# An earlier router, a shared bias split and one more weight place in a hybrid attention and mixture-of-experts block

## The reference

```python
h = x
h = h + hybrid_mixer(rms_norm(h, norm_mix_g), w_in, ..., w_out)   # two attentions, gated, then @ w_out
hn = rms_norm(h, norm_ffn_g)                                     # [256, 1024]
h = h + moe_ffn(hn, w_router, b_router, w_gate_up, b_gate_up, w_down, b_down)

def moe_ffn(xf, ...):
    logits = xf @ w_router + b_router                            # [256, 32]
    top_vals, top_idx = lax.top_k(logits, 4)
    gates = softmax(top_vals)
    # for each expert e, on the tokens that chose it:
    hgu = xb @ w_gu[e] + b_gu[e]                                 # 1024 -> 2048
    gate, up = min(hgu[:, :1024], 7), clip(hgu[:, 1024:], -7, 7)
    y = ((up + 1) * gate * sigmoid(1.702 * gate)) @ w_down[e] + b_down[e]
    # the gate-weighted y is added to the rows of its tokens
```

## Time and profile before

| | |
|---|---|
| median of 3 runs | 1224.87 us (1224.17 to 1225.32) |
| the profiled execution's own time | 1224.58 us |
| its span in the profile | 1223.0 us |
| PE busy | 1146.1 us (94%) |
| DVE busy | 277.8 us (23%) |
| ACT busy | 113.1 us (9%) |
| POOL busy | 33.0 us (3%) |
| moved by DMA | 435.75 MB, mean 356 GB/s |

### The profile page before, as it was taken

One profiled execution on the slowest core, in us unless ns is written; L12 is line 12 of the kernel. 1 busy time (PEld: TensorE's weight loads), 2 busy tenths in 40 slices (PEclk: granted clock), 3 DMA queues, 4 the chain that ended last, 5 costly groups with the idle time before them and its releaser, 6 DMA issues.

```text
span 1223.0 us, 12848 instructions
## 1 busy us (share of the span) xinstructions
PE 1146.1 (94%) x5681; PEld 553.6 (45%) x5681; DVE 277.8 (23%) x590; ACT 113.1 (9%) x206; POOL 33.0 (3%) x23
## 2 busy tenths in 40 slices
PE   6959999979999999999999978999999999999996
PEld 3656878554444444444444324444443333333331
DVE  1297332332111112221111111211111111111111
ACT  1102542010000000000000000000000000000000
POOL 1170000000000000000000000000000000000000
PEclk9979999968999999999999997999999999999999
DMA  7535336367999999999999999999999999999994
GB/s 231 168 138 216 129 138 275 142 275 292 373 418 417 417 418 416 418 417 417 417 417 417 417 417 417 416 418 417 417 417 417 417 417 417 416 417 417 417 417 199
DMA packets 87560, 435.75 MB, mean 356 GB/s; under 512 B 8688, under 2 KB 9872, under 8 KB 54640
## 3 DMA queue, kind: packets, MB, share of 16 engines
q1 hardware_dynamic: 87376, 434.83, 87.9%
q0 software_dynamic: 96, 0.08, 0.2%
q10 hardware_dynamic: 32, 0.01, 0.0%
HBM read 433.84 MB, written 1.05 MB: 356 GB/s over the span
## 4 chain that ended last, share of the span: by engine, by line
PE 63%; DMA 25%; DVE 4%; SPq 3%; issue 2%; ACT 1%; POOL 0%; DVEq 0%; POOLq 0%
PE Pp L682 25%; DMA ring<-in_w_gate_up 16%; PE Bp L697 12%; PE Bp L669 7%; DMA qkv<-in_w_gate_up 6%; PE Pp L456 5%; PE Pp L444 4%; PE Ap L711 3%; SPq L317 3%; PE Pp L609 2%; DMA XT<-in_w_gate_up 2%; PE Ap L620 1%; PE Pp L676 1%; PE Bp L689 1%; DVE ring L891 1%
## 5 line engine op out<-in xcount | busy, mean ns | idle before, releaser
L682 PE MATMUL Pp<-ring,OBT 128*64 128x512 f32 x1360 | 308.9, 603 | 14.4 <-DMA ring<-in_w_gate_up 14.4
L682 PEld LDWEIGHTS Pp<-ring,OBT 128*64 128x64 f32 x1360 | 95.6, 138 | 214.3 <-issue 166.0
L1086 DVE TENSOR_SCALAR G<-Pp 128x512 f32<-128x512 f32 x32 | 22.1, 691 | 674.1 <-PE Pp L682 674.1
L697 PE MATMUL Bp<-ring,G 128*64 128x512 f32 x688 | 152.8, 596 | 0.9 <-DVE G L1097 0.9
L669 PEld LDWEIGHTS Bp<-cst,XR 128*128 128x128 f32 x1024 | 122.6, 199 | 31.0 <-issue 31.0
L669 PE MATMUL Bp<-cst,XR 128*128 128x64 f32 x1024 | 127.2, 285 | 5.4 <-issue 4.4
L697 PEld LDWEIGHTS Bp<-ring,G 128*64 128x64 f32 x688 | 47.5, 137 | 90.7 <-issue 89.7
L456 PE MATMUL Pp<-XT,unit 128*128 128x256 f32 x384 | 85.9, 383 | 0.0
L682 PE MATMUL Pp<-unit,OBT 128*64 128x512 f32 x352 | 78.9, 594 | 2.5 <-DMA unit<-in_w_gate_up 2.4
L456 PEld LDWEIGHTS Pp<-XT,unit 128*128 128x128 f32 x384 | 72.7, 192 | 11.0 <-issue 1.1
L697 PE MATMUL Bp<-unit,G 128*64 128x512 f32 x320 | 70.9, 595 | 0.0
(11 more groups left out here) (191 smaller groups left out, 673.8 us busy)
## 6 DMA issues: line engine op xcount, KB each, us to landing
ring<-in_w_gate_up SPq DMA_DIRECT2D x170, 1024.0 KB, 20.7
ring<-in_w_down SPq DMA_DIRECT2D x86, 1024.0 KB, 25.4
unit<-in_w_gate_up SPq DMA_DIRECT2D x44, 1024.0 KB, 21.2
unit<-in_w_down SPq DMA_DIRECT2D x40, 1024.0 KB, 24.8
qkv<-in_w_gate_up SPq DMA_DIRECT2D x21, 1024.0 KB, 21.0
XT<-in_w_gate_up SPq DMA_DIRECT2D x21, 1024.0 KB, 19.2
unit<-in_w_in SPq DMA_DIRECT2D x8, 2048.0 KB, 7.9
ring<-in_w_out SPq DMA_DIRECT2D x2, 2048.0 KB, 12.9
```

The costliest lines, as they stand in the source:

```text
L682: last = mm((Gps, Ups)[q // 2][64 * (q % 2):64 * (q % 2) + 64, :], xT[:, k, :], w[:, q * 512:(q + 1) * 512], start=False, stop=k == KC - 1 ...
L697: last = mm(Yps[64 * hf:64 * hf + 64, :], hT[:, k % 4, k // 4, :], w[:, half * 1024 + hf * 512:][:, 0:512], start=k == 0, stop=k == KC - 1 ...
L1086: V.tensor_scalar(gm, Gps, LIMIT, None, ALU.min).then_inc(d_gm, 1)
```

## The change

1. **Router on the unnormed sum.** `turn_h` turns X itself, not a normed copy. The gain is multiplied once into the router weights, on POOL (`g_neg` = -0.5 times the gain). The factor of the norm (`nrm`, one number for a token, from `root_correction`, in which the factor -2 is left) is multiplied into the logits and into the one-hot of the gather. ACT alone empties the transposes.
2. **Order.** Block 0 is turned, multiplied by the router weights, routed and ranked between and inside the last out-projections (the fourth is cut in two halves by c); half of its gather follows right behind. `route` finds the chosen experts with `match_replace`; the gates are computed later (`gates`, behind the first `take_expert`), and the rank products use bf16 tables.
3. **Bias split** on ACT (four copies, one over 96 partitions) and DVE (three subtractions), out of `BG`, which is the memory of `XR`, loaded before unit 3. POOL keeps two new small instructions.
4. **One place more.** `BG` becomes place 18 of the ring, and piece (1, 8) is loaded into it right after unit 8. The output is written from X.

```diff
-PLACES = 18
+PLACES = 19
...
+        BG = XR[:, :, :].rearrange("p b n -> p (b n)")
...
+                if u == 2:
+                    sp.wait_ge(m_xt, 2)
+                    for s in range(3):
+                        sp.dma_start(BG[32 * s:32 * s + 32, :], b_gate_up[0]).then_inc(in_b, 16)
                 if u == 3:
-                    for s in range(3):
-                        sp.dma_start(W2[32 * s:32 * s + 32, :], b_gate_up[0]).then_inc(in_b, 16)
...
+                if u == 8:
+                    sp.wait_ge(bias_ok, 2)
+                    load_piece(1, 8)
...
             inverse_root(18, 2)
-            pool.wait_ge(in_b, 48)
...
+            pool.wait_ge(in_c, 16)
+            nc.gpsimd.tensor_copy(tab[:, :, :], strict_ones).then_inc(g_tab, 1)
+            pool.wait_ge(in_r, 16)
+            pool.wait_ge(a_gn, 2)
+            nc.gpsimd.tensor_tensor(WR[:, :, :], WR[:, :, :], g_neg.unsqueeze(2).to_broadcast([P, KC, NE]), ALU.mult)\
+                .then_inc(g_wr, 1)
...
             out_projection(0, 0)
             out_projection(0, 1)
+            turn_h(0, 0)
             out_projection(1, 0)
-            turn_h(0)
-            out_projection(1, 1)
-            router_products(0)
-            turn_h(1)
-            router_products(1)
+            turn_h(0, 1)
+            out_projection(1, 1, 0, 4)
+            pe.wait_ge(g_wr, 1)
+            router_products(0, 0)
+            router_products(0, 1)
+            turn_h(1, 0)
+            out_projection(1, 1, 4, KC)
+            pe.wait_ge(g_tab, 1)
+            pe.wait_ge(v_as, 1)
+            mm(Rps[:, 0, :], before, AS[:, 0, :], start=True, stop=True, skip_group_check=True).then_inc(m_rk, 1)
+            router_products(1, 0)
+            turn_h(1, 1)
+            pe.wait_ge(d_oh, 1)
+            gather_block(Tps, 0, 0, 4)
+            router_products(1, 1)
+            mm(Rps[:, 1, :], every, AS[:, 0, :], start=False, stop=False, skip_group_check=True)
+            mm(Rps[:, 2, :], every, AS[:, 0, :], start=False, stop=False, skip_group_check=True)
+            gather_block(Tps, 0, 4, KC)
+            pe.wait_ge(v_as, 2)
+            mm(Rps[:, 1, :], before, AS[:, 1, :], start=False, stop=True, skip_group_check=True)
+            mm(Rps[:, 2, :], every, AS[:, 1, :], start=False, stop=True, skip_group_check=True).then_inc(m_rk, 1)
             pe.wait_ge(z_ok, 1)
             for bank in range(4):
                 mm(Ap[:, bank, :], zero[:, 0:P], zero[:, P:], start=True, stop=False, skip_group_check=True)
...
+            pe.wait_ge(bias_ok, 2)
+            biases()
+            pe.wait_ge(d_oh, 2)
+            gather_block(Tps, 1, 0, KC).then_inc(m_ga, 1)
...
+            dve.wait_ge(a_bsp, 1)
+            for q in (1, 2):
+                r = slice(32 * q, 32 * q + 32)
+                V.tensor_tensor(BG[r, :], BG[r, :], bias3[r, :], ALU.subtract).then_inc(v_bsp, 1)
+            dve.wait_ge(a_bsp, 2)
+            V.tensor_tensor(BG[64:96, :], BG[64:96, :], bias3[64:96, :], ALU.subtract).then_inc(v_bsp, 1)
             dve.wait_ge(a_half, 4)
...
+            add_residual(1, 0)
+            sum_squares(1, 0)
+            guard_sum(1)
+            root_correction(0)
+            route(0)
+            add_residual(1, 1)
+            rank_block(0)
+            select_block(0, RK[:, 0, 0:1]).then_inc(d_oh, 1)
+            sum_squares(1, 1)
+            mean_square(1)
+            root_correction(1)
+            route(1)
+            rank_block(1)
+            select_block(1, RK[:, 0, 1:2]).then_inc(d_oh, 1)
...
+            evacuate((TM[:, 0, QI:QI + 512], 0, 512, HSCALE))
+            act.wait_ge(in_b, 48)
+            A(bias3[:, :], BG[0:3 * NE, :], ACT.Copy).then_inc(a_bsp, 1)
+            evacuate((TM[:, 1, QI:QI + 512], 0, 512, HSCALE))
+            act.wait_ge(v_bsp, 2)
+            A(bias3[64:96, :], BG[64:96, :], ACT.Copy).then_inc(a_bsp, 1)
+            evacuate_keys(0)
+            A(bias3[32:64, :], BG[32:64, :], ACT.Copy).then_inc(a_bsp, 1)
+            evacuate_keys(1)
+            act.wait_ge(a_bsp, 3)
+            act.wait_ge(v_bsp, 3)
+            A(bias3[64:96, :], BG[64:96, :], ACT.Copy).then_inc(bias_ok, 1)
```

More of the change, by code:

```diff
@@ L52 @@
 TAKEN = -3e38
+NEVER = 3e38
 HSCALE = HD ** -0.5
@@ L355, in _ @@
             load_piece(1, 7)
-            for s in range(8, PIECES):
+            for s in range(9, PIECES):
                 load_after_release(1, s)
@@ L400, in _ @@
             inverse_root(18, 2)
-            pool.wait_ge(in_b, 48)
[L403 to L419, removed]
+            pool.wait_ge(in_c, 16)
[4 more added lines that the diff above has]
+                .then_inc(g_wr, 1)
+            for b in range(TB):
+                pool.wait_ge(v_ms, 3 + b)
+                nc.gpsimd.tensor_tensor(sm[:, 40 + b:41 + b], sm[:, 20 + b:21 + b], mhalf[:, 0:1], ALU.pow)\
+                    .then_inc(p_rt, 1)
         @block.tensor
@@ L611, in _, with out_projection @@
                 last.then_inc(m_mg, 1)
-            def out_projection(b, hf):
-                for c in range(KC):
+            def out_projection(b, hf, c0=0, c1=KC):
+                for c in range(c0, c1):
                     if b == 0 and hf == 0:
@@ L621, in out_projection @@
                               urows(12 + c // 4)[:, c % 4, hf * 512:(hf + 1) * 512], start=c == 0, stop=c == KC - 1)
[L622 to L636, removed]
+                if c1 == KC:
+                    last.then_inc(m_wo, 1)
@@ L637, in router_products, with turn_h @@
+            def turn_h(b, i):
+                pe.wait_ge(v_hs, 2 * b + i + 1)
+                bank = Bp[:, i, :] if b == 0 else Ap[:, i, :]
+                for k in range(4 * i, 4 * i + 4):
+                    last = tr(bank[:, (k % 4) * P:(k % 4 + 1) * P], X[:, b, k * P:(k + 1) * P], ident)
+                last.then_inc(m_xt, 1)
+            def router_products(b, i):
+                pe.wait_ge(a_xt, 5 + 2 * b + i)
+                for k in range(4 * i, 4 * i + 4):
                     last = mm(Pp[:, 0, b * NE:(b + 1) * NE], XT[:, k, b * P:(b + 1) * P], WR[:, k, :],
-                              start=k == 0, stop=k == KC - 1)
@@ new lines, in _, with gather_block @@
+            out_projection(1, 1, 0, 4)
[9 more added lines that the diff above has]
+            turn_h(1, 1)
+            def gather_block(out_bank, b, k0, k1):
+                for k in range(k0, k1):
+                    last = mm(out_bank[:, k * SLOTS:(k + 1) * SLOTS], X[:, b, k * P:(k + 1) * P], OH[:, b, :],
+                              start=b == 0 and k == 0, stop=b == 1, skip_group_check=True)
@@ L761, in expert @@
                     pe.wait_ge(a_gt, e)
-                biases()
+                    biases()
                 for k in range(KC):
@@ L1134, in expert @@
                 turned_expert(e)
-            select_expert(0)
             take_expert(0)
+            for b in range(TB):
+                last = gates(b)
+            last.then_inc(v_gp, 1)
+            dve.wait_ge(v_gp, 1)
             for e in range(BREAK):
                 expert(e)
+            dve.wait_ge(v_rk, 1)
             most = dve.value_load(CNT[0:1, 0:1], min_val=0, max_val=SEQ)
```

179 lines of the change are left out of this document (98 added, 81 removed).

## The result

The changed kernel was executed four times: 1192.72, 1192.66, 6668.68 and 1194.05 us. The median of all four is 1193.38 us. The forecast was 1193.9 us, range 1187 to 1207.

The account below looks back on a forecast made before the run. The weight stream plus a tail was taken to bound the kernel. W 12.1, the hole at 270 12.8, the hole at 305 3.3 and one piece more 2.5 sum to 30.7 us: 1224.6 to 1193.9, range 1187 to 1207.

Parts of the forecast that it names:

- The bound: Whole kernel: its end is the end of the weight stream, flat at 417 GB/s, plus a tail; PE's 94% is no bound.
- W: Moment of `m_wo` 4, when SP issues seven pieces: 249.05 us before, forecast 236.9, 12.1 us earlier, bounds 0 to 14.5.
- The stall at 75 us: PE idles 12.76 us before its transposes, waiting for DVE's rotated keys; it and 1.8 us of slowness go, 14.5 us.
- rival A: The stream starts no earlier: something other than DVE holds PE between 75 and 98 us or later; 1208.4 us, chance 0.10.
- The bias split's place: Biases behind unit 2 land at 27.5 us; keys emptied by 36.3, needed at 36.56; cost 0, bounds 0 to 3.
- What moves in front of W: Router products of block 0 (1.87 us) and half a block's transposes (0.5 us) precede W, making it 2.4 us later.
- The hole at 270: Stream empty from about 270 to 283 us, awaiting expert 0's release; an earlier release closes it, 12.8 us.
- at 305: Stream slow from 300 to 315 us, waiting for expert 1; eight queued pieces close it, 3.3 us, bounds 0 to 3.3.
- one piece more: Piece (1, 8) is moved at about 120 us, so 13 pieces instead of 12 are there at W: 2.5 us.
- first release: PE frees its first piece behind W at W + 11, at most W + 17; before it was 32.6 us after.
- Rival C: Slower: PE becomes the bound, waiting for DMA sooner and falling to the half clock in most experts; 1239 us, chance 0.05.
- The tail: From the last gate-and-up piece, started when it lands, to the kernel's end: keeps its 24.1 us.

Follow-up runs that it names:

- z4_branch: The changed kernel with its overflow branch for crowded experts always taken (condition over 0 tokens instead of over 64): 5885.07 us in one execution.
- x2_18_places: The changed kernel without the place more (18 places, piece (1, 8) loaded after its release): 1197.65 us.
- y3_delay: The changed kernel with 60 idle bf16 products on PE in front of the expert biases, after W: 1218.54 us.
- y4_pool_late: The kernel before, but POOL starts its bias split only when DVE's rotated keys are done: 1209.86 us, 0.988 of before.
- x1_split_alone: The kernel before with only the new bias split on ACT and DVE, biases loaded behind unit 2: 1212.44 us, 0.990 of before.
- x4_repeat: The changed kernel again, unaltered, as a base on its chip: 1195.74 us, 0.978 of before.
- x3_three_early: The changed kernel with three of the seven pieces of W, (1, 4) to (1, 6), issued before W: 1192.46 us.
- y1_keys_first: The changed kernel, but ACT empties the keys of block 0 before its second copy of the biases: 1192.75 us.
- z2_early: The changed kernel with ACT emptying keys before its second bias copy and three pieces issued before W: 1189.54 us.
- z3_all_again: The changed kernel with keys emptied first, three pieces before W, zeroing moved behind the first gate-and-up and expert biases behind the second block's gather: 1190.50 us.

## Why the prediction was right, step by step

**The bound.** Right. Late in the kernel the stream is flat at 417 GB/s in every profile but that of z4_branch, and each change of W, of a hole or of a piece came through to the end: x2_18_places 2.7 us of stream for a piece of 2.51, y3_delay 23.8 us for a delay of 25.2.

**The stall at 75 us**, 14.5 us. Right in size and cause. PE starts the unit product behind it at 85.14 instead of 98.05, 12.9 us earlier, although it was 1.65 us late from the start: 14.6. y4_pool_late shows the cause by itself, with the same 14.6. The two POOL instructions that remain, priced at 1.2 us of DVE at worst and nothing for PE, held DVE for about half a microsecond: its small product at 62.50 took 0.55 us, where one without POOL beside it (18 columns too, at 63.29) took 0.18. Nothing after 98 us took the gain back, so rival A did not happen: from this unit product to W it is 151.0 us in x1_split_alone as in the kernel before.

**The bias split's place**, cost 0, slack 0.3 us. This is the step that was mis-sized. The term that failed is the landing of the biases: 27.5 us was forecast, and in the profiles with this split ACT's copy starts between 28.6 and 30.5. The forecast took about 200 GB/s; the changed kernel's one-microsecond windows from 25 to 28 us have 178, 164 and 98. The rest of the step held (two subtractions 4.59 us, 4.56 expected), so the bank was ready at 37.5 to 39.3 and not at 36.3. The cost was hidden in the first profile and 0.94 us in x4_repeat; in x1_split_alone, x2_18_places, x3_three_early and y3_delay PE waited 2.4 to 3.6 us and then ran the unit 1.7 to 2.7 us longer, at the half clock (0.50 in x3_three_early from 38 to 44 us). Bounds of 0 to 3 stood beside the step; the worst case, x3_three_early, is 6.3, twice that. y1_keys_first takes the step off the path.

**What moves in front of W**, 2.4 us. From the unit product at 85.14 to W it is 153.2 us, before 151.0: 2.2.

**The hole at 270**, 12.8 us, and **at 305**, 3.3 us, with **one piece more**, 2.5: together 18.6, measured 19.5 (and 19.4 in x4_repeat and y1_keys_first). Of this x2_18_places gives 2.7 to the place. x1_split_alone keeps the hole and the first release at W + 32.7 with W early, so the rest is due to the router, parts 1 and 2 of the change together. No run separates the two: what the router on the unnormed sum would bring in the old order, or the new order with normed rows, is not shown. The first release was forecast at W + 11, and at most W + 17 with the half clock; it was W + 15.1. The clock did fall: the gather of 16 products took 3.68 us, twice what was counted, in a window with a clock of 0.50. That the hole closed all the same was no luck: the stream has work for 20 us there, and this margin was worked out beforehand.

**Rival C**, PE as the bound. It did not happen. In the later part PE waits for DMA in every expert, as before, and the stream is never empty. The fall at the branch of expert 16 came again (granted clock 0.50 from 705 to 710 us, the stream at 415 GB/s) and cost nothing.

**The tail**, unchanged at 24.1. It was 22.4 in the profile of the result, where PE kept its clock (1.00 from 1170 to 1185 us, against 0.76 and 0.56 in the first two windows of five microseconds in x4_repeat), and 22.5 in z2_early; in the other ten profiles of the experiments it lies between 24.0 and 25.4. This 1.7 us is luck.

**How close the number is.** In the profile W gained 10.7 us instead of 12.1, the stream 19.5 instead of 18.6, and the tail 1.7 instead of nothing: 32.0 instead of 30.7. The lack in W is PE's own late start at 38.21, which the forecast had no term for, and the tail about cancels it. On the chip of x4_repeat the gain was 28.2 us (1195.74 against 1223.92). So the mechanism and the sum are right within some 2 us, and the agreement of the first runs with the forecast to about one microsecond (1192.72 against 1193.9) is in part luck.

## What to carry to other kernels

When a transfer stream is the bound, count its start, its holes and what is already loaded, and treat every engine's work as lateness of a release: free up to the slack that the queued work gives it, paid nearly in full beyond. Emptying PSUM for PE should stand in front of any work on the same engine that waits for a transfer; a slack of 0.3 us in a sum of five estimated terms is none. Work on GpSimd is not free because GpSimd is idle: look at which VectorE instructions with two SBUF inputs run beside it. And look at several executions: one profile can hide a wait behind an accident of that execution, as the first one did at 37 us.

## What the runs showed of the hardware

- A POOL instruction with SBUF inputs holds up a DVE instruction with two SBUF inputs for about its whole length (0.69 to 4.45 us beside a subtraction of 4.67, and 3.61 to 18.53 us for seven of them beside seven of POOL), and leaves MAX8 beside it as it is (0.42 us).
- In y3_delay PE was busy without a break for 25.2 us with bf16 products of one partition; the granted clock, which had fallen by 250 us, stayed at 0.50 until 280. It was at 0.95 in the window from 280 us, under the gate-and-up products. Whether it is the one partition or the type is not shown.
- PE's pace until about 22 us differs between executions of the same code: the first 64 products with `w_in` take 19.39 us in z3_all_again, 21.08 in the kernel before and 22.31 in the changed kernel. In the kernel before the windows show a granted clock of 0.50 from 17 to 20 us. In the other two they read 1.00 throughout, so the clock is a likely cause but not a shown one.
- This goes into the time in full. The third unit starts, where PE had no wait, at 35.04 (z3_all_again), 36.94 (y1_keys_first), 38.21 (the changed kernel) and 38.36 us (z2_early), and W follows 200.1 us later in all four. These 3.3 us are most of the spread of single executions.
- The three bias loads, 256 KB into 32 partitions each, moved at 179 GB/s in the window of the earlier trace rows and at 178 and 164 in two windows of the changed kernel, less than half of the 417 of the weight pieces.
